# Two column strips for the sample tokens' value projections and for the forget gate

## The reference

```
z = jnp.einsum('bsd,de->bse', h, w_in)
logf = jax.nn.log_sigmoid(fg.astype(jnp.float32) + b_forget.astype(jnp.float32))
```

## Time and profile before

| what | value |
|---|---|
| median of three runs | 756.88 us |
| profiled execution, span | 771.2 us |
| TensorE busy | 630.2 us, 82% |
| VectorE busy | 306.5 us, 40% |
| ScalarE busy | 189.5 us, 25% |
| GpSimd busy | 144.0 us, 19% |
| mean DMA rate | 302 GB/s |
| chain that ended last | PE 62%, DMA 19%, DVE 10%, ACT 4% |

### The profile page before, as it was taken

One profiled execution on the slowest core, in us unless ns is written; L12 is line 12 of the kernel. 1 busy time (PEld: TensorE's weight loads), 2 busy tenths in 40 slices (PEclk: granted clock), 3 DMA queues, 4 the chain that ended last, 5 costly groups with the idle time before them and its releaser, 6 DMA issues.

```text
span 771.2 us, 11399 instructions
## 1 busy us (share of the span) xinstructions
PE 630.2 (82%) x4436; PEld 387.5 (50%) x4436; DVE 306.5 (40%) x778; ACT 189.5 (25%) x485; POOL 144.0 (19%) x179
## 2 busy tenths in 40 slices
PE   4779999997878898888989994388888777878870
PEld 2355546653565665565658794354444343434420
DVE  1411311222865444655452157434442334242307
ACT  1202000101854344334332043111111111111134
POOL 3030300211012222332200002022222121212130
PEclk9979999999999999999899995599999999999965
DMA  9998768973416689998797049579799999999542
GB/s 306 408 368 302 249 255 307 361 297 121 193 51 256 245 338 403 362 372 328 303 399 297 33 162 385 218 295 420 304 417 415 418 415 418 418 416 416 208 140 76
DMA packets 48607, 233.23 MB, mean 302 GB/s; under 512 B 6452, under 2 KB 6637, under 8 KB 32052
## 3 DMA queue, kind: packets, MB, share of 16 engines
q1 hardware_dynamic: 30242, 145.80, 47.5%
q0 software_dynamic: 15344, 79.96, 27.2%
q10 hardware_dynamic: 2978, 6.88, 2.6%
HBM read 220.51 MB, written 17.87 MB: 309 GB/s over the span
## 4 chain that ended last, share of the span: by engine, by line
PE 62%; DMA 19%; DVE 10%; ACT 4%; issue 2%; SPq 1%; ACTq 1%; POOL 1%; POOLq 0%; DVEq 0%
DMA ring<-w 12%; PE ps L1887 11%; PE ps L1605 9%; PE ps L1712 8%; PE ps L1609 5%; PE ps L1808 5%; DMA ring<-w_in 4%; PE ps L1732 4%; PE ps L1755 3%; DVE work L1399 2%; PE ps L1723 2%; PE ps L1896 2%; PE ps L1504 2%; PE ps L1964 1%; DMA work<-scr_h 1%
## 5 line engine op out<-in xcount | busy, mean ns | idle before, releaser
L1887 PE MATMUL ps<-ring,work 128*64 128x256 f32 x960 | 120.1, 407 | 17.6 <-DMA ring<-w 14.5
L1887 PEld LDWEIGHTS ps<-ring,work 128*64 128x64 f32 x960 | 74.0, 146 | 55.3 <-issue 29.1
L1712 PE MATMUL ps<-cst,ring 128*128 128x128 f32 x512 | 68.2, 291 | 16.7 <-ACT work L760 7.9
L1605 PE MATMUL ps<-xh,ring 128*128 128x320 f32 x256 | 72.9, 443 | 7.4 <-DMA ring<-w_in 7.4
L1712 PEld LDWEIGHTS ps<-cst,ring 128*128 128x128 f32 x512 | 60.3, 149 | 25.8 <-ACT work L760 11.0
L1399 DVE TENSOR_SCALAR work<-work 128x128 f32<-128x128 f32 x32 | 15.7, 490 | 141.9 <-ACT work L850 141.9
L1605 PEld LDWEIGHTS ps<-xh,ring 128*128 128x128 f32 x256 | 49.2, 195 | 29.3 <-DMA ring<-w_in 7.6
L1178 DVE COPY work<-ps 128x512 f32<-128x512 f32 x64 | 43.7, 691 | 38.5 <-PE ps L1712 38.4
L1896 PE MATMUL ps<-ring,work 128*64 128x512 f32 x240 | 56.8, 593 | 0.7 <-ACT work L854 0.7
L602 POOL DMA_INDIRECT scr_y<-work,y_row x32 | 31.5, 984 | 112.1 <-DVE work L1410 103.1
L760 ACT COPY work<-ps 128x512 f32<-128x512 f32 x64 | 36.5, 591 | 51.1 <-PE ps L1712 51.1
(11 more groups left out here) (372 smaller groups left out, 850.0 us busy)
## 6 DMA issues: line engine op xcount, KB each, us to landing
ring<-w SPq DMA_DIRECT2D x90, 1024.0 KB
ring<-w_ada SPq DMA_DIRECT2D x4, 4096.0 KB, 14.0
ring<-w_ada SPq DMA_DIRECT2D x4, 2048.0 KB, 16.7
ring<-w_in SPq DMA_DIRECT2D x2, 4096.0 KB, 34.5
ring<-w_in SPq DMA_DIRECT2D x2, 2048.0 KB
ring<-w_out SPq DMA_DIRECT2D x1, 4096.0 KB, 16.2
work<-w SPq DMA_DIRECT2D x3, 1024.0 KB, 8.0
scr_y<-work POOLq DMA_DIRECT2D x1, 2304.0 KB, 16.4
```

The lines of the kernel that those rows point to most:

```text
L1605: last = mm(ps[r % 4][:, 0:NT], wv[:, k, col:col + P], hT[:, k, :], start=(k == 0), stop=(k == KC - 1))
L1712: last = tp(ps[4 + k % 4][:, t * P:(t + 1) * P], kd[:, q, t, c * P:(c + 1) * P], ident)
L1887: last = mm(o, h_cur[:, par, c, :], w[:, c, f], start=(c == 0), stop=(c == KC - 1))
```

## The change

Rounds 10 and 21 (`SAMPLE_VALUES`) run as two strips: for each of the eight chunks, two matmuls of 256 columns with the same 64 sample tokens stationary. The first half of the value columns goes to rows 0 to 63 of the bank, the second to rows 64 to 127, both in columns 0 to 255. The evacuation is two copies of 64 x 256 in place of one operation on 64 x 512, on ScalarE for round 10 and on VectorE for round 21; the second brings the rows back to partitions 0 to 63.

The forget gate's product runs as two strips of 160 tokens, in rows 0 to 7 and 32 to 39 of its bank. VectorE copies the two strips into `lfT`, then adds the bias in place, behind a wait; the semaphore `fg_v` is now raised by the second copy.

```diff
-            n = TILES[t][1]
-            return v_tok[0:n, g, t, :], ps[r % 4][0:n, :], 1.0
+            return v_tok[:, g, t, :], ps[r % 4][:, :], 1.0
+
+        def sample_values(r):
+
+            g = PROJ[r][3][0]
+            return [(v_tok[0:NS, g, 2, 256 * hf:256 * hf + 256], ps[r % 4][NS * hf:NS * hf + NS, 0:256])
+                    for hf in range(2)]
...
+                if r == SAMPLE_VALUES[0]:
+                    (d0, s0), (d1, s1) = sample_values(r)
+                    nc.scalar.copy(d0, s0)
+                    nc.scalar.copy(d1, s1).then_inc(S["proj_a"], 1)
+                    return
...
+                if r == SAMPLE_VALUES[1]:
+                    (d0, s0), (d1, s1) = sample_values(r)
+                    nc.vector.tensor_copy(d0, s0)
+                    nc.vector.tensor_copy(d1, s1).then_inc(S["proj_v"], 1)
+                    return
...
-            ts(lfT[:], ps[4][0:H, 0:NT], bfg[:, 0:1], None, ALU.add).then_inc(S["fg_v"], 1)
+            nc.vector.tensor_copy(lfT[:, 0:NT // 2], ps[4][0:H, 0:NT // 2])
+            nc.vector.tensor_copy(lfT[:, NT // 2:], ps[4][32:32 + H, 0:NT // 2]).then_inc(S["fg_v"], 1)
             v.wait_ge(S["fg_v"], 1)
+            link(ts(lfT[:], lfT[:], bfg[:, 0:1], None, ALU.add))
...
                 for k in range(KC):
-                    last = mm(ps[4][0:H, 0:NT], wfg[:, k, :], hT[:, k, :], start=(k == 0), stop=(k == KC - 1))
+                    for hf in range(2):
+                        last = mm(ps[4][32 * hf:32 * hf + H, 0:NT // 2], wfg[:, k, :],
+                                  hT[:, k, hf * NT // 2:(hf + 1) * NT // 2], start=(k == 0), stop=(k == KC - 1))
...
+                    elif r in SAMPLE_VALUES:
+                        for hf in range(2):
+                            last = mm(ps[r % 4][NS * hf:NS * hf + NS, 0:256], hT[:, k, NP:],
+                                      wv[:, k, col + 256 * hf:col + 256 * hf + 256],
+                                      start=(k == 0), stop=(k == KC - 1))
```

More of the change, by code:

```diff
@@ L363, in trunk_kernel @@
                 + [(True, 4, j * P, 12 + j) for j in range(4)] + [(False, 4, W, (1, t)) for t in range(3)])
+        SAMPLE_VALUES = (10, 21)
         def proj_evac(r):
```

## The result

| kernel | median | runs | ratio to before, 95% interval |
|---|---|---|---|
| before | 757.0 us | 18 | |
| changed | 752.93 us | 18 | 0.995 [0.9933, 0.9966] |
| changed, repeated, with its own 35 runs of before (756.74 us) | 752.6 us | 12 | 0.9938 [0.9912, 0.9963] |

The change makes the kernel 3.8 us faster (0.5% of 757.0 us; the interval is 2.6 to 5.1 us). The forecast was 6.8 us. The sign is right and the time lies in the forecast's range of 745.5 to 754 us, but the gain is a little over half of the one forecast, which lies outside the interval. The profiled execution of the changed kernel has a span of 750.2 us, and its own time was 751.94 us.

The account below looks back on a forecast made before the run. TensorE was taken to bound the projection stage, with its gain arriving undiminished at the end. 6.48 (rounds) + 2.0 (gate) - 0.1 (tiling) - 0.16 (evacuation) - 1.4 (wait) = 6.8 us off 756.88: 750.1 us, range 745.5 to 754.

Parts of the forecast that it names:

- What bounds the stage: Projection stage: TensorE is busy throughout, so time cut from its pieces moves the rest unless something else ends a wait.
- Sample rounds: Rounds 10 and 21 on TensorE: two strips take 3.63 us instead of 6.87, saving 6.48 us for both.
- The gate: Forget gate's product on TensorE: two strips take 2.40 us instead of 4.40, saving 2.0 us.
- Rival 2: Forget gate: strips don't pay because weight loads are exposed; saving 5.4 to 3.9 us, 751.5 to 753.0 us; chance 0.08.
- rival 3: Rounds and gate: strips take turns with weight loads exposed, slower than before, 768.8 us (757.2 with loads hidden); chance 0.04.
- Changes of tiling: TensorE's switches of strip width: charged 0.1 us in all, with 0 and 0.6 us as ends.
- Evacuation: Round 21's two VectorE copies cost 0.16 us more, ends 0 and 0.3; round 10's and the gate's extra work is hidden.
- The wait at `ada_mm(3)`: TensorE waits for this product's load, delayed by ScalarE's transfers that round 10 releases: 1.4 us, between 0 and 2.0.
- Rival 4: After the projection stage: gain lost later, when a key or expert load releases the next stage; 754 to 757 us; chance 0.09.
- The load for `ada_mm(2)`: Waits for round 8's first matmul and keeps its relation: both move by the gate's 2.0 us.
- Rival 1: At `ada_mm(3)`: the load lands in time, wait 0; saving 8.2 us, 748.7 us; chance 0.24.

Follow-up runs that it names:

- the kernels with the cures: Changed kernel with ScalarE's transfers held until the `ada_mm(3)` load landed, with `ada_mm(3)` and `ada_mm(4)` one round later, or both: gains 12.2, 11.6, 10.0 us.
- The controls: Kernel before, no strips, with `ada_mm(3)` and `ada_mm(4)` one round later, or with ScalarE's transfers held: ratios 1.0006 and 1.000.

## Why the prediction was right or wrong

**What bounds the stage: right.** Every cut of TensorE's work that met no load moved the stage's end by its own size (round 21 alone 3.40, round 10 with later products 3.41 us).

**Sample rounds: right, the saving a little under-counted.** 3.63 us forecast from an expert's row; 3.63 us measured for round 21 and 3.60 for round 10, 32 entries each. The forecast took the saving from 6.87 us, the rounds of 128 tokens, but the two rounds that it cut took 7.01 and 7.02, so they gave 3.41 and 3.39 us and not 3.24. **The gate: right.** Forecast 2.40 us with 2.2 and 5.28 as ends, measured 2.28, 142 ns a pair. Its weight loads are hidden, at the median 90 ns each:

```profile
L1555 PEld LDWEIGHTS ps<-xh,wfg x32: 85/90/90, 57.0 to 58.9; 128*8 128x8 f32 x32
L1555 PE MATMUL ps<-xh,wfg x32: 299/299/303, 57.0 to 59.1; 128*8 128x160 f32 x32
```

32 loads of 90 ns would be 2.9 us; loads and products together fit into 2.28. So rivals 2 and 3 are out. By the Trainium skill, "TensorE: Matmul & The Clock Gate", The mechanism, loads overlap matmuls in flight only when the row group differs; that isn't what these strips of columns do.

**Changes of tiling: right in size, read off the wrong rows.** 0.1 us was charged and none shows: the gate ends at 59.37, where the next piece starts, and both sample rounds take an expert's time. But the 0.14 us are not what a product in 32-row strips costs the round behind it. Round 21, which stands behind transposes, took 7.02 us too, and the rounds of 128 tokens or columns behind such a product take 7.06 us for 6.87 and 4.50 for 4.31, 0.19 us more.

**Evacuation: right.** Two copies on VectorE, 0.42 + 0.44 us on the chain for 0.69 before: 0.17 us, forecast 0.16. ScalarE's two took 366 and 369 ns, off the path. The gate's longer work on VectorE is hidden: VectorE still idles for 2.81 us before round 3's evacuation.

**The wait at `ada_mm(3)`: right cause, wrong size, and a part missed.** This is the term that failed. The forecast took 1.4 us, between 0 and 2.0. The measured terms are 3.23 us of idle TensorE and 1.51 us more for the product, 4.7 us in all, against the 3.41 that round 10 gives. That is 3.3 us more than forecast. The other terms differ by little: 0.3 us more from the two rounds, 0.1 from the gate, 0.1 from the change of tiling, and 0.25 less at `ada_mm(2)`, so that 6.8 - 3.3 + 0.5 - 0.25 gives the 3.8 measured.

That the time still fell into the range is in part luck. With the wait at its upper end the sum is 6.2 us, 750.7 us; the range went on to 754 us for scatter and for rivals 2 and 4, neither of which happened. Rival 2's 751.5 to 753.0 us hold the measured median, but its mechanism is not the one at work.

The size of the wait: the estimate halved the load's rate from 111.2 us on, which made it 2.6 us late, and took less than that by choice. ScalarE's and SyncE's queues in the changed kernel, microseconds 109 to 110, 112 to 113, 113 to 114, 114 to 115 and 116 to 117 (packets, MB, share; they answer to the earlier trace rows):

```profile
q1 hardware_dynamic: 69, 0.28, 68.7%
q10 hardware_dynamic: 67, 0.13, 33.3%
...
q1 hardware_dynamic: 74, 0.30, 73.5%
q10 hardware_dynamic: 70, 0.12, 31.1%
...
q10 hardware_dynamic: 78, 0.32, 78.0%
q1 hardware_dynamic: 38, 0.11, 28.4%
...
q10 hardware_dynamic: 52, 0.43, 100.5%
q1 hardware_dynamic: 9, 0.02, 4.3%
...
q10 hardware_dynamic: 366, 0.37, 105.6%
q1 hardware_dynamic: 2, 0.01, 2.0%
```

The load kept about two thirds of the rate from 109 to 113 us (0.28 to 0.30 MB/us, not 0.2). The packets say why: 69 against 67 in a microsecond, 74 against 70, one for one, and the load's are twice as large. By the Trainium skill, "DMA: Bandwidth & Descriptors" (Queues, rings and completion order), each DMA engine takes turns between its queues packet by packet; the trace agrees in these microseconds. So the bulk of the load was moved by 114 us, earlier than the estimate had it. But a load isn't landed until its last packets are: 9 of them in one microsecond and 2 in another trickled through until 117 us in between ScalarE's (52 of 8 KB in the first, 366 of 1 KB in the other). A rate was the wrong model; the tail decided, and the load landed 17.6 us after its issue, 3.6 us later than before. The forecast's margin of 0.6 us off that leaves 3.0, near the 3.23 measured. That ScalarE's transfers make the tail is shown, since it is gone when they are held; why the last packets are so late isn't: from 114 us on the counts are no longer one for one. Nor is the tail round 10's alone: with only the gate in strips, and with the gate and round 21, the load landed after 15.9 us, which the margin covered.

The part missed: the forecast said that the clock would stay at 1.00 all through the stage, though it had TensorE wait for 1.4 us. A wait on the path was priced by its length alone, without what it does to the work behind it.

**The load for `ada_mm(2)`: its relation right, its slack not looked at.** It had 0.4 us to spare before. Its wait was 0.1 us in the changed kernel, with 0.1 us more for the product behind it, and 1.2 us in the profile with the gate alone.

**Rival 1** (the load in time, 8.2 us) is what the kernels with the cures show in their stage: 8.2 to 8.6 us, or 8.0 to 8.4 with the longer evacuation. **Rival 4** (lost later) did not happen: the middle stretch is 212.3 to 214.5 us whatever the projection did, except for the first profile of before (229.7 us) and the repeat of the changed kernel (216.1 us).

**Open.** The kernels with the wait removed gained 10.0 to 12.2 us where their projection gained 8.2 to 8.6. The controls show that it isn't the edits by themselves. In the profiles most of it lies between the start of the output projection and the end of the first two experts' hidden product: 92.1 to 93.3 us in these three, 93.5 to 95.4 in the eleven others. The second profile of before has there (chain of waits)

```profile
462.96 6.71 DMA scr_h<-work,slotu
...
484.19 8.83 PE ps L1887 x64
```

and the kernel with the transfers held

```profile
458.01 4.13 DMA scr_h<-work,slotu
...
476.64 7.14 PE ps L1914 x64
```

The landing of sorted rows took 4.1 to 6.7 us over the profiles, and the first two experts' 64 instructions 7.14 or 8.83 us. The two values are two clocks: over these instructions the granted clock is 1.00 in all eight profiles with 7.14 us and 0.81 in all six with 8.83. The first profile of before (7.14 us) and that of round 21 alone (6.72 and 8.83 us) show that both values occur without the cures. Whether an earlier start of that stage makes the better values likelier, or chance did, wasn't settled.

## What to carry to other kernels

Before a piece of work is shortened, look at what was hidden behind it: a load that is issued in front of it and wanted right after it loses of its margin what the piece gives up. Then look at what the end of the piece sets off, because that starts earlier too and can take bandwidth from that same load. A wait on TensorE of some 3 us is to be priced with the slow stretch that follows (here 1.5 us); and moving one line in the order of the stream puts other work in front of it. When a load shares the DMA engines with another queue, budget its landing by its last packets and not by a mean rate.

## What the runs showed of the hardware

- The 4 MB load for `ada_mm(3)` landed 17.2 to 18.2 us after its issue when another queue's transfers (0.64 and 1 MB, and from 14.4 us on 0.64 MB more) were issued from 4.4 us after it on, 13.8 to 15.9 us when they were issued 7.7 us after it, and 13.5 to 13.9 us when they were held. In the changed kernel its bytes were delayed little, its last packets by 3 us and more.
- After 3.2 us without work in the projection stage TensorE ran at half the clock for 2.5 us and more; the same product took 5.08 us and not 3.57. In two other profiles it took 5.07 us after 2.9 us idle and 5.33 after 3.45.
- Two strips of 8 stationary columns, 160 moving, take 142 ns a pair, where one instruction of 320 takes 275.
- A round with 64 tokens stationary took 7.01 or 7.02 us in one piece of 512 columns and 3.60 or 3.63 us in two strips of 256.
- The first two experts' hidden product took 7.14 us at a granted clock of 1.00 and 8.83 us at 0.81.
- A single profile can be an outlier of its kernel: 771.2 us against 756.3, with the excess in one stage.
